# Layer 1's head products in three passes, the network seams prepared ahead, and the modulation sums moved

## What is computed

```python
for l in range(2):
    mod = silu(c) @ ada_w[l] + ada_b[l]          # for c and c_ctx, 6 parts of 1024
    hl, hc = modulate(x_lat, g, mod[0], mod[1]), modulate(x_ctx, ...)   # rms norm, gain, shift
    mix = even_mixer(hc, hl, ...) if l == 0 else odd_mixer(hc, hl, ...)
    x_lat = x_lat + mod[2] * (mix @ w_out[l])
    x_lat = x_lat + mod[5] * conv_ffn(modulate(x_lat, g2, mod[3], mod[4]), up, conv, down)
    # layer 0 does the same for x_ctx
```

## Time and profile before

| | us |
|---|---|
| median of 3 timed runs (lowest, highest) | 1763.13 (1762.99, 1764.4) |
| the profiled execution, whole | 1762.85 |
| its span on the core | 1761.6 |
| TensorE busy | 1642.3 (93%) |
| VectorE busy | 964.4 (55%) |
| ScalarE busy | 645.8 (37%) |
| GpSimd busy | 466.8 (26%) |

### The profile page before, as it was taken

How to read it: one execution, slowest core, us unless ns; L and a number is a source line. 1 busy time by engine, 2 the same in 40 slices (tenths; PEclk the granted TensorE clock), 3 DMA queues, 4 the chain that set the end, 5 groups by cost and what they waited for, 6 DMA issues and landing times.

```text
span 1761.6 us, 24231 instructions
## 1 busy us (share of the span) xinstructions
PE 1642.3 (93%) x9336; PEld 1317.7 (75%) x9336; DVE 964.4 (55%) x1910; ACT 645.8 (37%) x1230; POOL 466.8 (26%) x384
## 2 busy tenths in 40 slices
PE   7999999889999989989989899899999999999888
PEld 5555565357888878856657899898999988878777
DVE  4488888543222277747764688564544544233821
ACT  2442333033333332223332555444444444134511
POOL 1012202016555500022220111014555555013401
PEclk9999999999999999999999999999999999999999
DMA  9333323322222345514332455453344333325131
GB/s 349 116 120 132 107 100 129 108 95 96 96 97 98 103 149 197 182 41 166 134 138 91 156 189 181 157 180 121 131 146 138 136 133 121 127 88 179 61 125 36
DMA packets 63825, 231.16 MB, mean 131 GB/s; under 512 B 7408, under 2 KB 8432, under 8 KB 63456
## 3 DMA queue, kind: packets, MB, share of 16 engines
q1 hardware_dynamic: 60800, 218.65, 36.5%
q0 software_dynamic: 2192, 6.29, 1.1%
q10 hardware_dynamic: 720, 4.68, 0.7%
HBM read 228.55 MB, written 1.05 MB: 130 GB/s over the span
## 4 chain that ended last, share of the span: by engine, by line
PE 84%; DVE 9%; ACT 3%; issue 3%; POOL 1%; DMA 0%; DVEq 0%; ACTq 0%; POOLq 0%
PE ps L232 17%; PE ps L250 10%; PE ps L252 10%; PE ps L251 10%; PE ps L1194 4%; PE ps L1195 3%; PE ps L1196 3%; PE ps L1679 3%; PE ps L725 3%; PE ps L240 3%; PE ps L715 2%; PE ps L379 2%; PE ps L618 2%; PE ps L294 1%; PE ps L1494 1%
## 5 line engine op out<-in xcount | busy, mean ns | idle before, releaser
L259 ACT ACTIVATE weights_rounded<-ring 128x1024 fp32r<-128x1024 f32 x194 | 203.2, 1053 | 104.9 <-PE ps L1196 104.8
L250 PE MATMUL ps<-h_hi,weights_rounded 128*128 128x512 f32 (+1 forms) x656 | 221.3, 337 | 5.0 <-POOL weights_rest L271 2.9
L251 PE MATMUL ps<-h_lo,weights_rounded 128*128 128x512 f32 (+1 forms) x656 | 221.2, 337 | 0.0
L252 PE MATMUL ps<-h_hi,weights_rest 128*128 128x512 f32 (+1 forms) x656 | 221.0, 337 | 0.0
L265 DVE TENSOR_TENSOR weights_rest<-ring,weights_rounded 128x1024 fp32r<-128x1024 f32 x128 | 178.7, 1397 | 73.5 <-ACT weights_rounded L259 73.3
L232 PE MATMUL ps<-h,ring 128*128 128x512 f32 (+1 forms) x496 | 195.8, 551 | 7.0 <-DVE h L471 7.0
L271 POOL TENSOR_TENSOR weights_rest<-ring,weights_rounded 128x1024 fp32r<-128x1024 f32 x66 | 158.0, 2395 | 162.2 <-ACT weights_rounded L259 162.2
L232 PEld LDWEIGHTS ps<-h,ring 128*128 128x128 f32 x496 | 95.0, 194 | 99.9 <-issue 91.2
L1165 DVE SCALAR_TENSOR_TENSOR scratch<-ps,vectors,scratch 128x510 f32<-128x510 f32 (+1 forms) x88 | 54.1, 615 | 194.6 <-ACT scratch L1125 194.6
L250 PEld LDWEIGHTS ps<-h_hi,weights_rounded 128*128 128x128 f32 x656 | 124.9, 190 | 18.4 <-POOL weights_rest L271 3.3
L1194 PE MATMUL ps<-hid_rounded,weights_rounded 128*128 128x512 f32 (+1 forms) x352 | 123.4, 351 | 14.5 <-DVE hid_rest L1264 14.5
(11 more groups left out here) (295 smaller groups left out, 3421.3 us busy)
## 6 DMA issues: line engine op xcount, KB each, us to landing
ring<-in_up SPq DMA_DIRECT2D x88, 512.0 KB, 3.5
ring<-in_ada_rest SPq DMA_DIRECT2D x80, 512.0 KB, 3.7
ring<-in_a_in SPq DMA_DIRECT2D x80, 512.0 KB, 3.5
ring<-in_down SPq DMA_DIRECT2D x44, 512.0 KB, 3.7
ring<-in_even SPq DMA_DIRECT2D x20, 512.0 KB, 3.7
ring<-in_ada_first SPq DMA_DIRECT2D x16, 512.0 KB, 8.0
ring<-in_wout SPq DMA_DIRECT2D x16, 512.0 KB, 3.5
ring<-in_odd SPq DMA_DIRECT2D x16, 512.0 KB, 4.9
```

Source lines behind the costliest of these rows:

```text
L250: te.matmul(bank[:, 0:n], wh[:, k, :], hi(k), start=k == 0, stop=False)
L251: te.matmul(bank[:, 0:n], wh[:, k, :], lo(k), start=False, stop=False)
L252: ins = te.matmul(bank[:, 0:n], wl[:, k, :], hi(k), start=False, stop=k == KD - 1)
L259: sc.activation(pair[0], place(*key), ACT.Copy).then_inc(*mark("rounded", *key))
```

## The change

Five things, in the order of the program:

- **Modulation sums** go 6 per `even` round (was 8; the pair in front of the softmax maxima is the one that goes), 4 in layer 0's `wout` (was 6), 20 in layer 0's `up` (was none; one after every second convolution), 20 in `down` (was 22), 2, 2, 1 and 1 in the `odd` rounds (was 5 each), 6 in layer 1's `wout` (was none).
- **Start of `up`**: product 3 gets a fourth pair of buffers (`UP_THIRD`), filled before it is needed, and in both layers DVE makes all the rests of `up`, none are left to POOL.
- **From `up` to `down`**: the first two `down` tiles and their inputs are split in the last two steps of `up`, and TensorE begins `down` on banks 4 to 7 while banks 0 to 3 are still being convolved.
- **`odd_pre` and `odd`** use split products throughout. Their input is split by a chain like that of `up` (`act_odd_h`, `dve_odd_h`), the first three products run abreast, the value products are made with features on the partitions and turned by four transposes (`pe_turn_values`) between two ACT copies. POOL makes the rests of the first three and of every product 2, DVE the others.
- **Order within a round**: product 0 of the next round runs between the global and the near weighing, product 1 ahead of the rope, product 2 behind it; the near weighing turns into four banks of its own, the global maxima come ahead of the key's norm, two exponentials ahead of its logarithm.

The diff, cut to its core (in `pe_odd_pre` the three abreast are a loop like that of `up`; `act_odd_h` and `dve_odd_h` repeat L1111, L1150 and L1146 on 16 pieces of 256 columns):

```diff
-        ada_tiles(8 * i + 6, 8 * i + 7, 8 * i, 8 * i + 1)
+        ada_tiles(6 * i + 4, 6 * i + 5, 6 * i, 6 * i + 1)
...
+    UP_ADA = 20
+    ODD_ADA = [(68, 69), (70, 71), (72,), (73,)]
...
+            if layer and b < 6:
+                ada_tiles(74 + b)
...
-            tile(("up", layer, j), f"up{layer}", j, "rest_pool" if layer == 0 else "rest", "up", layer, j)
+            tile(("up", layer, j), f"up{layer}", j, "rest", "up", layer, j)
+            if layer == 0 and j % 2 and j // 2 < UP_ADA:
+                ada_tiles(28 + j // 2)
...
+            if layer == 0 and j < UP_ADA:
+                ada_tiles(28 + UP_ADA + j)
...
+    def odd_on_pool(i, s):
+        return s == 2 or (i == 0 and s == 0)
...
-        dve_ada(8 * i + 4)
-        dve_ada_bias(8 * i, 8)
+        dve_ada_bias(6 * i, 6)
...
-            if layer and b == 6:
+            if b == 6:
                 for j in range(FIRST):
-                    dve_rest(("up", layer, j), pair(j), up_free(layer, j))
+                    dve_rest(("up", layer, j), up_pair(j), up_free(layer, j))
...
-        if layer == 0:
-            for j in range(FIRST):
-                pool_rest(("up", layer, j), pair(j), up_free(layer, j))
...
+    UP_THIRD = (rounded("up_rounded_3", "big", 9216, D), rounded("up_rest_3", "big", 10240, D))
+
+    def up_pair(j):
+        return UP_THIRD if j == FIRST else pair((j if j < FIRST else j - 1) % PAIRS)
+
     def up_free(layer, j):
-        return [at("product", "up", layer, j - PAIRS)] if j >= PAIRS else \
-            ([at("product", "down", 0, FB - PAIRS + j)] if layer else [])
+
+        if j == FIRST:
+            return [at("mixed_near", 3)] if layer else [at("mixed_heads", AH - 1)]
+        if j > FIRST:
+            return [at("product", "up", layer, j - (PAIRS if j > FIRST + PAIRS else PAIRS + 1))]
+        return [at("product", "down", 0, FB - 1)] if layer else []
+
+    def down_pair(j):
+        return pair((j + 1) % PAIRS)
+
+    def up_rounds(layer, j):
+
+        return {-1: [FIRST], 0: [], 1: [FIRST + 1], 2: []}.get(j, [j + 2] if j + 2 < 2 * FB else [])
...
+            if j >= 2 * FB - 2:
+                act_down_first(layer, j - 2 * FB + 2)
...
+            if layer == 0 and g and fb < UP_ADA:
+                dve_ada(28 + fb, 1)
...
+            if e == (3 if j < 2 else KD - 1):
...
-        te.wait_ge(*at("convolved", layer, 2 * FB - 1))
-        for j in range(FB - 3):
+        for j in range(2):
+            ready(j)
+            for e in range(4, KD):
+                block(j, e)
+        for e in range(4):
+            te.wait_ge(*at("convolved", layer, 2 * FB - 4 + e))
+            for j in range(2):
+                block(j, e)
+        for j in range(2, FB - 3):
...
+    def act_down_first(layer, j):
+
+        n = TOK if layer == 0 else SEQ
+        act_round(("down", layer, j), down_pair(j), down_free(layer, j))
+        sc.wait_ge(*at("hidden", layer, j))
+        if j >= 4:
+            sc.wait_ge(*at("product", "down", layer, j - 4))
+        sc.activation(HID_T[j % 4][0][:, 0:n], BIG[:, j * n:(j + 1) * n],
+                      ACT.Copy).then_inc(*mark("hidden_rounded", layer, j))
...
+    def dve_down_rest(layer, j):
+        n = TOK if layer == 0 else SEQ
+        dve_rest(("down", layer, j), down_pair(j), down_free(layer, j))
+        ve.wait_ge(*at("hidden_rounded", layer, j))
+        hi, lo = (x[:, 0:n] for x in HID_T[j % 4])
+        ve.tensor_tensor(lo, BIG[:, j * n:(j + 1) * n], hi.bitcast(F32),
+                         ALU.subtract).then_inc(*mark("hidden_rest", layer, j))
...
+            if layer == 0 and j >= FB - 2:
+                x = j - FB + 2
+                act_round(first_odd(x), pair_first_odd(x), [at("hidden_rest", 0, FB - 8)])
...
+    ODD_FIRST = 3
+    ODD_BANKS = [1, 2, 6]
...
+    def odd_pair(i, s):
+        return pair((4 * i + s - 1) % PAIRS)
+
+    def odd_free(i, s):
+        n = 4 * i + s - PAIRS
+        return [at("product", "odd", n // 4, n % 4)] if n >= 1 else [at("product", "down", 0, FB - 1)]
...
+    def pe_turn_values(key, bank):
+
+        te.wait_ge(*at("copied", *key))
+        for t in range(4):
+            ins = te.transpose(bank[:, 128 * t:128 * t + 128], VFM[:, 128 * t:128 * t + 128], ident)
+        ins.then_inc(*mark("turned", *key))
...
     def pe_odd(i):
+
         glob, near = units1(i, 0), units1(i, 1)
-        pe_product(("odd", i, 0), BANK[6], SEQ, hk(256, SEQ))
-        pe_product(("odd", i, 1), BANK[7], SEQ, hk(256, SEQ))
         if i:
             te.wait_ge(*at("mixed_global", i - 1))
         pe_norm(("odd", i, 0), u1, BANK[5], SEQ)
         if i:
-            te.wait_ge(*at("mixed_near", i - 1))
-        pe_product(("odd", i, 2), BANK[4], TOK, hk(0, TOK))
+            pe_odd_product(i, 1, BANK[7], CTX, SEQ)
         te.wait_ge(*at("norm_log", "odd", i, 0))
         pe_rope(("odd", i), at("normed", "odd", i, 0), q1, ROPE1, BANK[5])
+        if i:
+            te.wait_ge(*at("mixed_near", i - 1))
+        pe_odd_product(i, 2, BANK[4], 0, TOK)
         te.wait_ge(*at("rope_sin", "odd", i))
         pe_norm(("odd", i, 1), u2, BANK[5], SEQ)
         te.wait_ge(*at("roped", "odd", i))
@@ -1363,52 +1511,69 @@
         te.wait_ge(*at("norm_log", "odd", i, 1))
         pe_norm(("odd", i, 2), u1, BANK[5], TOK)
         te.wait_ge(*at("normed", "odd", i, 0))
-        pe_product_tokens(("odd", i, 3), BANK[6], TOK, hk(0, TOK))
+        pe_odd_product(i, 3, BANK[6], 0, TOK)
         te.wait_ge(*at("normed", "odd", i, 1))
         te.wait_ge(*at("normed", "odd", i, 2))
         pe_scores(near, [[at("exp", "odd", i, 0, 0), at("exp", "odd", i, 0, 2)],
                          [at("exp", "odd", i, 0, 1), at("exp", "odd", i, 0, 3)]])
+        pe_turn_values(("odd", i, 3), BANK[6])
         pe_weigh(WK(i, 0), packs(glob), [7, 6], PT1, (5, 5), [[], [at("v2_copied", i)], [at("norm_log", "odd", i, 2)]])
-        pe_weigh(WK(i, 1), packs(near), [6, 7, 0, 1], PT1, (4, 4), [[], [], [], [], []])
+        if i < 3:
+            pe_odd_product(i + 1, 0, BANK[6], CTX, SEQ)
+        pe_weigh(WK(i, 1), packs(near), [0, 1, 2, 3], PT1, (4, 4), [[], [], [], [], []])
...
-        act_square(("odd", i, 0), u1, BANK[6], SEQ)
+        if i == 0:
+            sc.wait_ge(*at("normed", *KEY1))
+            act_square(("odd", i, 0), u1, BANK[6], SEQ)
+        act_norm(("odd", i, 0), u1, BANK[5], SEQ)
+        act_odd_round(i, 3)
         if i == 0:
             sc.wait_ge(*at("roped", *KEY1))
         act_square(("odd", i, 1), u2, BANK[7], SEQ)
-        act_norm(("odd", i, 0), u1, BANK[5], SEQ)
+        act_odd_round(i + 1, 0)
         sc.wait_ge(*at("normed", "odd", i, 0))
         act_square(("odd", i, 2), u1, BANK[4], TOK)
         act_norm(("odd", i, 1), u2, BANK[5], SEQ)
+        act_exps(glob[0:2])
         act_norm(("odd", i, 2), u1, BANK[5], TOK)
-        act_exps(glob)
+        act_exps(glob[2:4])
+        act_odd_round(i + 1, 1)
         sc.wait_ge(*at("product", "odd", i, 3))
+        sc.activation(VFM, BANK[6], ACT.Copy).then_inc(*mark("copied", "odd", i, 3))
+        act_exps(near[0:2])
+        sc.wait_ge(*at("turned", "odd", i, 3))
         sc.activation(v2, BANK[6], ACT.Copy).then_inc(*mark("v2_copied", i))
-        act_exps(near[0:2])
         weigh_copies(sc, 1, WK(i, 0), packs(glob), [7, 6], PT1)
         act_exps(near[2:4])
-        weigh_copies(sc, 1, WK(i, 1), packs(near), [6, 7, 0, 1], PT1, [at("weighed", WK(i, 0), j) for j in (0, 1)])
+        act_odd_round(i + 1, 2)
+        if i < 3:
+            sc.wait_ge(*at("normed", "odd", i, 2))
+            act_square(("odd", i + 1, 0), u1, BANK[6], SEQ)
...
-        dve_ada(60 + 5 * i, 3)
         dve_norm(("odd", i, 0), BANK[6], SEQ, gq1[:, 0:1], q1, u1)
-        dve_ada(63 + 5 * i)
+        dve_rope(("odd", i), ROPE1, BANK[5], u3)
+        dve_odd_rest(i, 3)
+        dve_odd_rest(i + 1, 0)
+        dve_ada(ODD_ADA[i][0], len(ODD_ADA[i]))
         if i == 3:
-            dve_ada_bias(60, 20)
-        dve_rope(("odd", i), ROPE1, BANK[5], u3)
+            dve_ada_bias(ODD_ADA[0][0], 6)
         dve_norm(("odd", i, 1), BANK[7], SEQ, gq1[:, 1:2], q2, u2)
+        dve_maxima(glob)
         dve_norm(("odd", i, 2), BANK[4], TOK, v(V_NA + 1), k2, u1)
-        dve_maxima(glob)
         dve_probs(glob)
         dve_maxima(near[0:2], free=[at("bias_masked", i, 3)])
         weigh_copies(ve, 0, WK(i, 0), packs(glob), [7, 6], PT1)
         dve_maxima(near[2:4])
+        dve_odd_rest(i + 1, 1)
...
+        pool_odd_rest(i + 1, 2)
...
```

More of the change, by code:

```diff
@@ new lines, in pe_odd_product, with odd_parts, act_odd_h @@
+    def pe_odd_product(i, s, bank, lo, n):
+        pe_product3(("odd", i, s), odd_pair(i, s), bank, n, odd_hi(lo, n), odd_lo(lo, n),
+                    "rest_pool" if odd_on_pool(i, s) else "rest")
+    def odd_parts():
+        for k in range(KD):
+            for s in range(2):
+                yield k, s, slice(k * TOK + 256 * s, k * TOK + 256 * s + 256)
+    def act_odd_h():
+        act_rsqrt((1, 0), TOK)
```

(4 more changed lines are left out.)

182 lines of the change are left out of this document (115 added, 67 removed).

## The result

| | before | after |
|---|---|---|
| median (lowest, highest), us | 1763.06 (1761.78, 1764.4) | 1713.74 (1712.09, 1717.75) |
| span of the profiled execution, us | 1761.6 | 1713.5 |
| TensorE / VectorE / ScalarE / GpSimd busy | 93 / 55 / 37 / 26% | 94 / 62 / 39 / 24% |

What follows compares the result with a forecast made beforehand. TensorE was taken as the bound (84% of the chain), through its work and idle time. Six terms, 6.0 + 15.0 + 18.3 + 1.6 + 0.8 + 4.8 = 46.5 us, off 1762.85 gave 1716 us; 8-in-10 range 1701 to 1732.

Steps and rivals of the forecast that it cites:

- part 1: In `up` of both layers, a fourth buffer pair removes the waits at product 3; 6.0 us, bounds 4.5 and 6.6.
- Part 2: Between `up` and `down`, early splitting and bank order remove both stalls and the low clock behind; 15.0 us, bounds 10.7 and 15.0.
- Part 3: In `odd_pre` and `odd`, split products cost TensorE less than float32 ones; 18.3 us, called the firmest term.
- Part 4: Waits in `odd` rounds: 16.4 us recovered less losses to value path, sums and POOL's rest; net 1.6, bounds -14.8 and +16.4.
- 5, entry: At the entry of `odd`, TensorE's idle time falls from 4.79 to 4.03 us; 0.8 us, bounds -1 and +1.5.
- part 6: In `even`, softmax maxima start earlier without the pair of sums, cutting TensorE's 2.00 us wait; 4.8 us, bounds 0 and 8.
- POOL's lock: In `odd`, POOL's rest of the next product 2 collides with DVE's near scaling; 2 us in three rounds, 6.0 lost.
- the rounds do not close up: Rival, in `odd`: the lock and longer value path eat the recovered waits and more, DVE arrives last; 1728 us, chance 0.19.
- The clock stays up: Rival: fewer gaps in `even` and `odd` spare the low clock there too; 1705 us, chance 0.15.
- Seams move: Rival: `down`'s third block or `up`'s fifth product waits instead, leaving 8 of 21 us won; 1729 us, chance 0.10.
- Split products no cheaper: Rival: split products in `odd` cost no less, for weight loads or the lower clock; 1734 us, chance 0.03.
- DVE as the bound of layer 0's `up`: Rival: DVE, waiting for POOL, exceeds TensorE's 10.9 us per product pair; at 14 a pair 1778 us, chance 0.04.

Runs made afterwards that it cites:

- e2: Changed kernel with `up`'s product 3 split only after product 0 is done, in both layers, so no fourth pair; 1719.13 us against 1713.74.
- e1: Changed kernel with the pair of modulation sums ahead of the softmax maxima put back in each `even` round; 1724.12 us against 1713.74.
- e5: Changed kernel with DVE, not POOL, making the rest of product 2 of `odd` rounds 2 to 4; 1710.25 us, stage 160.56 against 166.82.
- e6: Changed kernel with the `odd` values copied once, without the four transposes and second copy (wrong layout); 1709.34 us, stage 161.27.
- e13: Changed kernel with ACT's second copy of the `odd` values moved ahead of the first two near exponentials; 1706.94 us, stage 162.07.
- e7: Changed kernel without the six modulation sums of the `odd` rounds and their loads (part of layer 1's modulation wrong); 1710.75 us, stage 164.04.
- e8: Changed kernel with product 0 of the next `odd` round behind the near weighing, not between the weighings; 1729.79 us, stage 184.97.
- e11: Changed kernel with split products of `odd_pre` and `odd` making two passes, not three (computation left out); 1708.39 us, stage 162.32.
- e12: Changed kernel with DVE scaling the context probabilities ahead of the division of the heads in `even`; 1712.44 us against 1713.74.
- e9: Changed kernel with mixer A's first three tiles prepared at blocks 10, 14 and 18 of layer 1's `down`, not 18, 19 and 20; 1708.44 us.

## Why the prediction came out right

| part | forecast | measured | from |
|---|---|---|---|
| 1, fourth product | 6.0 | 5.9 | `e2` |
| 2, `up` to `down` | 15.0 | 17 | both stages, 22.9, less part 1 |
| 3 and 4, `odd` | 19.9 | 17.6 | traces |
| 5, entry | 0.8 | 0.8 | traces, idle 4.79 to 4.03 |
| 6, `even` | 4.8 | 6.6 | traces; 11.0 by `e1` |
| sum | 46.5 | 47.9 of the spans' 48.1 | |

**Parts 1, 2 and 5** held: the stalls went whole, with the low clock behind them. Part 2 brought 2 us more than its upper bound. Some 0.7 of it belong to part 1, whose stall in `e2`, with DVE making the rest, is 2.21 us and not the 2.90 of before, with POOL. Another 0.7 are the 0.17 us by which each of the four brackets falls short of the distance between starts, which the sum left out. The rest, 0.6, is open.

**The total was luckier than its parts.** By `e1` part 6 was worth 11.0 us, not 4.8. The two traces show 6.6 of it, because the one after began its first round 2.9 us later and fell once to the low clock. Without that the trace would have come out some 4.5 us lower, further from 1716.

**Part 4's list** was nearly right item by item in size, though each size held some clock that the forecast had not counted. POOL's lock: 6.0 of waits forecast, 6.3 by `e5`, of which 4.3 is waiting and 2.0 clock; the longest scaling took 2.61 us, where I wanted 2.4. The Trainium skill ("SBUF — State Buffer", section "SBUF: two separate sides") says that DVE and GpSimd exclude each other on their shared ports; this run is the agreement, 3.92 us for four scalings beside POOL and 1.75 without. The value path: 4.8 forecast, 5.6 by `e6`; but I put it down to the turn, and it was ACT's order, 4.8 of it (`e13`). The modulation sums: 4.0 forecast, 2.8 by `e7`, one round instead of two, and half of it clock. What product 0 covers: 18.2 us by `e8`, of which 8.1 is clock, more than the whole 16.4 I had as recovered.

**Part 3** has the reason that failed. I called it TensorE's own work, which nothing hides, and the firmest term. Together with part 4 the size came out, but the two are not separable that way: in the changed kernel 25.8 us less product work make the stage only 4.5 us shorter (`e11`). Every product of a round is also the cover of somebody's chain, so a shorter product uncovers a wait and the clock falls with it. The rival that the rounds do not close up was thus partly true: the last three took 37.7, 35.0 and 32.1 us where I wanted 35 to 37 (the last has no next product 0 in it), with waits of 1.3 to 2.2 us left. What the split products alone would have given in the old order was not tried. Against the stage before, TensorE is busy 18.0 us less (163.08, now 145.05), the size of part 3, while the idle time only went from 22.15 to 21.78, 0.4 less with the entry's 0.8 in it, and the clock from 0.98 to 0.97: the rounds recovered no idle time in the sum, where part 4 had 1.6.

```profile
761.00:946.23 185.23, 163.08 (x886) 110.92 (x884) 122.92 (x282) 62.65 (x134) 44.35 (x62) 0.98 0.36 121
```

**Part 6** had the wait right (1.2 a round) and left out the clock (1.6 a round), the larger half. It also said that the wait ahead of the value products would shrink from 2.00 to 0.8; it stayed at 2.01. What shrank were the short waits between the transposes ahead of it and the start of the round's tail; behind the maxima comes the division, whose copies are still queued last, and behind those ACT's (`e12`).

**The rivals.** The clock stays up: true in `even` in three rounds of four, not in `odd`. Seams move: no. Split products no cheaper: no, product 0 of the third round took 2.98 us from start to start, against 3.5 in float32. DVE as the bound of layer 0's `up`: it is busy 190.55 of 241.04 us there, 8.7 a pair of products, and TensorE never waits, though DVE and POOL both take longer there. The sums' second operation took 1.54 us in the mean over all 80, against 1.26 before, and 2.07 for those in layer 0's `up`. The 1.05 us of POOL's product, which the forecast used for layer 0, is a mean over two shapes; taken apart, the 128x512 one of layer 0 took 1.29 us before and 2.15 after, and the 128x256 one of layer 1 no longer than before. Before, then after:

```profile
L1180 POOL TENSOR_TENSOR big<-scratch 128x512 f32<-128x512 f32 x22 | 28.3, 1287 | 84.5 <-DVE scratch L1168 84.5
...
L1204 POOL TENSOR_TENSOR big<-scratch 128x512 f32<-128x512 f32 x22 | 47.2, 2145 | 262.5 <-DVE scratch L1190 262.5
L1204 POOL TENSOR_TENSOR big<-scratch 128x256 f32<-128x256 f32 x22 | 17.1, 775 | 147.7 <-DVE scratch L1190 147.7
...
L332 DVE SCALAR_TENSOR_TENSOR ring<-ring,cond_rows 128x1024 f32<-128x1024 f32 x80 | 123.1, 1539 | 2.8
```

One place kept its stall, layer 1's `down` end, which the change didn't touch. It went with `e9`, and the rows beside POOL's three rests there (3.37 and 2.62 us on DVE, usually 1.23 and 0.42) point to the same lock.

## What to carry to other kernels

Price a removed wait together with the clock behind it: here the clock was more than half of what a short wait cost in `even`, and almost half of what an uncovered product cost in `odd`. When a stage is made of short products and chains of other engines, a product's length is also a cover, so ask for each one whose chain it hides before counting its saving as firm. Where POOL and DVE both have work on large tiles, put POOL's pieces where DVE waits, singly and not at the end of a stage, and look at the order in an engine's queue before blaming the steps themselves. Split each measured gain into idle time and clock before adding it to another: four gains here held the same fall of the clock.
